# Expert tiles of 32 rows on four column quarters of TensorE, moved on ScalarE's queue, in a hybrid diffusion layer with 16 routed experts

## What is computed

```python
def routed_moe(h, router_w, router_b, w1, w3, w2):
    ...  # sigmoid scores; one of 4 expert groups, then the top 2 of its 4 experts
    gate = jnp.sum(jax.nn.one_hot(idx, N_EXPERTS, dtype=F32) * w[..., None], axis=1).astype(h.dtype)
    out = jnp.zeros_like(h)
    for e in range(N_EXPERTS):                       # 16 experts, w1, w3: 1024x512, w2: 512x1024
        he = jax.nn.silu(h @ w1[e]) * (h @ w3[e])
        out = out + gate[:, e:e + 1] * (he @ w2[e])
    return out
```

## Time and profile before

| | us |
|---|---|
| median of three runs | 1959.97 |
| the profiled execution | 1965.64 |
| its span, first to last instruction | 1964.0 |
| span until the first matmul of the experts (L998) | 1590.4 |
| expert stage, to the end of the last `down` | 333.3 |
| gather, sum, norm and output after it | 40.3 |
| bytes moved in the whole span | 243.50 MB |

### The profile page before, as it was taken

One profiled execution on the slowest core, in us unless ns is written; L12 is line 12 of the kernel. 1 busy time (PEld: TensorE's weight loads), 2 busy tenths in 40 slices (PEclk: granted clock), 3 DMA queues, 4 the chain that ended last, 5 costly groups with the idle time before them and its releaser, 6 DMA issues.

```text
span 1964.0 us, 17655 instructions
## 1 busy us (share of the span) xinstructions
PE 1720.4 (88%) x6784; PEld 945.7 (48%) x6785; DVE 736.4 (37%) x1229; ACT 380.6 (19%) x651; POOL 266.8 (14%) x272
## 2 busy tenths in 40 slices
PE   4988899799789879999999999999999569999791
PEld 0553454355355344544545555446564236666460
DVE  1144644653754554600027774123143312222124
ACT  2321232132132121000123334101100201111111
POOL 0003412421430540000000000000000021111014
PEclk9999989899989889999999999999999879999896
DMA  9611101011021025621120111215205749887974
GB/s 315 253 40 43 43 22 43 4 61 43 1 86 43 0 78 217 219 85 45 49 79 0 43 44 43 86 44 184 86 0 215 264 155 372 308 297 257 379 268 141
DMA packets 108941, 243.50 MB, mean 124 GB/s; under 512 B 7913, under 2 KB 17134, under 8 KB 108882
## 3 DMA queue, kind: packets, MB, share of 16 engines
q1 hardware_dynamic: 86800, 180.59, 26.0%
q0 software_dynamic: 14128, 50.60, 7.4%
q10 hardware_dynamic: 7954, 11.50, 1.6%
HBM read 220.40 MB, written 22.28 MB: 124 GB/s over the span
## 4 chain that ended last, share of the span: by engine, by line
PE 74%; DVE 13%; ACT 4%; issue 3%; POOL 2%; DMA 2%; ACTq 1%; SPq 1%; DVEq 0%; POOLq 0%; PEldq 0%
PE psum L419 15%; PE psum L998 9%; PE psum L431 8%; PE psum L709 6%; PE psum L1023 4%; PE psum L596 4%; PE psum L423 4%; PE psum L824 3%; PE psum L654 2%; PE psum L622 2%; PE psum L493 2%; PE psum L441 2%; PE psum L858 1%; PE psum L756 1%; DVE arena L1621 1%
## 5 line engine op out<-in xcount | busy, mean ns | idle before, releaser
L419 PE MATMUL psum<-arena 128*128 128x512 f32 x688 | 315.2, 615 | 9.7 <-issue 4.0
L419 PEld LDWEIGHTS psum<-arena 128*128 128x128 f32 x688 | 133.3, 197 | 171.9 <-issue 164.1
L998 PE MATMUL psum<-arena 128*64 128x256 f32 x1664 | 190.5, 387 | 10.8 <-DMA arena<-exp_w_d 9.2
L998 PEld LDWEIGHTS psum<-arena 128*64 128x64 f32 x1664 | 144.7, 139 | 62.6 <-issue 29.0
L431 PE MATMUL psum<-arena 128*128 128x512 f32 x352 | 151.6, 592 | 0.0
L596 PE MATMUL psum<-arena 128*128 128x512 f32 x256 | 130.7, 641 | 1.2 <-ACT arena L1172 1.2
L709 PE MATMUL psum<-arena 128*128 128x512 f32 x256 | 111.6, 593 | 0.0
L431 PEld LDWEIGHTS psum<-arena 128*128 128x128 f32 x352 | 66.8, 190 | 83.3 <-issue 83.2
L1023 PE MATMUL psum<-arena 128*64 128x512 f32 x416 | 95.0, 596 | 6.1 <-ACT arena L1439 6.1
L2013 POOL TENSOR_TENSOR arena<-arena 128x512 f32<-128x512 f32 x40 | 49.5, 1247 | 359.4 <-ACT arena L1227 309.2
L2049 POOL TENSOR_TENSOR arena<-arena 128x512 f32<-128x512 f32 x64 | 82.6, 1294 | 103.0 <-ACT arena L1267 103.0
(11 more groups left out here) (340 smaller groups left out, 2096.6 us busy)
## 6 DMA issues: line engine op xcount, KB each, us to landing
arena<-exp_w_d SPq DMA_DIRECT2D x48, 2048.0 KB, 19.1
arena<-w_in_d SPq DMA_DIRECT2D x22, 2048.0 KB, 7.8
arena<-ada_w_d POOLq DMA_DIRECT2D x8, 2048.0 KB, 9.1
slots<-arena POOLq DMA_DIRECT2D x1, 8704.0 KB, 26.3
arena<-ada_w_d SPq DMA_DIRECT2D x4, 2048.0 KB, 23.4
arena<-ssd_proj_d SPq DMA_DIRECT2D x4, 2048.0 KB, 9.8
arena<-slots POOLq DMA_DIRECT2D x28, 256.0 KB, 6.4
slots<-arena POOLq DMA_DIRECT2D x54, 128.0 KB, 5.3
```

The source lines that it names most:

```text
L419: ins = mmul(ps[:, 0:T], slot[:, k, m * P:(m + 1) * P], src[:, k, C:NT], start=(k == 0), stop=(k == KD - 1))
L998: ins = mmul(ps[q * R:(q + 1) * R, 0:HF], XT[:, k, :], w[:, k, q * HF:(q + 1) * HF], start=(k == 0), stop=(k == KD - 1))
```

## The change

Tiles have 32 rows instead of 64. Four tiles' worth of partitions fit, so `up` and `down` use four column quarters of the array: quarter q streams columns q x 128 to (q+1) x 128 of w1 and, in the same call, of w3 (one view `w13` spans both buffers); psG goes, Silu reads the left 128 columns of psU and the product the right ones. `up` has 8 x 4 = 32 calls of 256 columns, `down` 4 x 4 = 16 calls of 256 columns.

A tile's rows lie on all 128 partitions as (quarter of the channels, row): `xrow` is 128 x 256 instead of 64 x 1024, and `ysb` 128 x 256 in place of 128 x 512. So two transposes turn a tile instead of eight, and one turns the activations instead of two.

Loads and stores of the rows move from GpSimd's queue to ScalarE's, into ScalarE's loop, behind its copy: one load and one store for each tile, the latter in one piece. Their side in HBM is a view with the quarter as its outermost dimension, `r (q c) -> q r c` with q = 4.

With 32 rows the experts take 3, 2, 3, 1, 5, 3, 3, 5, 2, 2, 1, 1, 1, 3, 3, 2 tiles, 40 in all. Core of the diff:

```diff
-ROWS_A_TILE = 64
-HF = FF // 2
-XTILES = 2 * T // ROWS_A_TILE + NE + 2
+ROWS_A_TILE = 32
+NQ = P // ROWS_A_TILE
+HF = FF // NQ
+DQ = D // NQ
+XTILES = 2 * T // ROWS_A_TILE + NE + 4
...
+        w13 = [view(off, (2, KD, FF)) for off in (wset0, 0, phase_base)]
...
             def up(p, j):
                 pe.wait_ge(S_("x_ready"), j + 1)
-                for i, (ps, name) in enumerate(((psG, "g_full"), (psU, "u_full"))):
-                    w = wmem[p][i].rearrange("p (k n) -> p k n", k=KD)
-                    for k in range(KD):
-                        for q in range(2):
-                            ins = mmul(ps[q * R:(q + 1) * R, 0:HF], XT[:, k, :], w[:, k, q * HF:(q + 1) * HF],
-                                       start=(k == 0), stop=(k == KD - 1))
-                    ins.then_inc(S_(name), 1)
+                for k in range(KD):
+                    for q in range(NQ):
+                        ins = mmul(psU[q * R:(q + 1) * R, 0:2 * HF], XT[:, k % 2, k // 2, :],
+                                   w13[p][:, :, k, q * HF:(q + 1) * HF], start=(k == 0), stop=(k == KD - 1))
+                ins.then_inc(S_("u_full"), 1)
             def turns(j):
                 pe.wait_ge(S_("xrow_in"), j * 16 + 32)
-                turn_x(0, KD - 3)
+                turn_x()
                 pe.wait_ge(S_("he_ready"), j + 1)
-                for i in range(HF // P):
-                    ins = nc.tensor.transpose(psH[:, i * P:(i + 1) * P], hg[:, i * P:(i + 1) * P], ident)
-                ins.then_inc(S_("h_turned"), 1)
-                turn_x(KD - 3, KD)
+                nc.tensor.transpose(psH[:, 0:P], hg, ident).then_inc(S_("h_turned"), 1)
...
+                for k in range(NQ):
+                    for q in range(NQ):
+                        ins = mmul(psD[q * R:(q + 1) * R, 0:DQ], heT[:, k, :],
+                                   w2[:, k, q * DQ:(q + 1) * DQ], start=(k == 0), stop=(k == NQ - 1))
...
+            quarters = lambda rows: slots[rows, :].rearrange("r (q c) -> q r c", q=NQ)
+            def load_x(rows):
+                act.dma_start(xrow[:, 0:DQ], quarters(rows)).then_inc(S_("xrow_in"), 16)
+            def send_y(rows):
+                act.dma_start(quarters(rows), ysb).then_inc(S_("y_sent"), 16)
...
             with act.Fori(0, n) as j:
-                act.wait_ge(S_("g_full"), j + 1)
-                run(sg, bank(("G",))[:, 0:HF], ACT.Silu).then_inc(S_("g_ready"), 1)
+                act.wait_ge(S_("u_full"), j + 1)
+                run(sg, bank(("U",))[:, 0:HF], ACT.Silu).then_inc(S_("g_ready"), 1)
                 act.wait_ge(S_("h_turned"), j + 1)
-                run(heT, bank(("H",))[:, 0:HF].rearrange("p (b t) -> p b t", t=P), ACT.Copy).then_inc(S_("heT_ready"), 1)
+                run(heT.rearrange("p q r -> p (q r)"), bank(("H",))[:, 0:P], ACT.Copy).then_inc(S_("heT_ready"), 1)
+                act.wait_ge(S_("x_turned"), j + 2)
+                load_x(bass.ds(j * R + 2 * R, R))
+                act.wait_ge(S_("y_ready"), j + 2)
+                send_y(bass.ds(j * R, R))
...
-            with pool.Fori(0, n) as j:
-                pool.wait_ge(S_("x_turned"), j + 2)
-                pool.dma_start(xrow[0:R, :], slots[bass.ds(j * R + 2 * R, R), :]).then_inc(S_("xrow_in"), 16)
-                pool.wait_ge(S_("y_ready"), j + 2)
-                send_y(bass.ds(j * R, R))
```

More of the change, by code:

```diff
@@ L252, in build @@
         g1row = alloc(D)
-        g2half = alloc(D // 2)
-        XT = alloc(KD, ROWS_A_TILE)
+        g2q = alloc(DQ)
+        XT = alloc(DQ // P, NQ, ROWS_A_TILE)
         assert top[0] <= phase_base
@@ L278, in build @@
         hg = alloc(HF)
-        heT = alloc(HF // P, P)
-        ysb = alloc(D // 2)
+        heT = alloc(NQ, ROWS_A_TILE)
+        ysb = alloc(DQ)
         junk2 = xrow
@@ L976, in _ @@
             R = ROWS_A_TILE
-            psG = open_(pe, ("G",), 1, 0, 1)
             psU = open_(pe, ("U",), 1, 1, 2)
@@ L981, in _, with turn_x @@
             psH = open_(pe, ("H",), 1, 4, 5)
[L983 to L988, removed]
+            def turn_x():
+                for i in range(DQ // P):
+                    ins = nc.tensor.transpose(psX[:, i * P:(i + 1) * P], xrow[:, i * P:(i + 1) * P], ident)
+                ins.then_inc(S_("x_turned"), 1)
             def up(p, j):
@@ L1039, in _ @@
             pe.wait_ge(S_("xrow_in"), 16)
-            turn_x(0, KD)
+            turn_x()
             pe.wait_ge(S_("tiles_known"), 1)
@@ L1433, in _ @@
             act.wait_ge(S_("tiles_known"), 1)
-            n = act.value_load(first_tile_i[0:1, NE:NE + 1], min_val=1, max_val=XTILES)
+            n = act.value_load(first_tile_i[0:1, NE:NE + 1], min_val=1, max_val=XTILES - 4)
+            R = ROWS_A_TILE
+            quarters = lambda rows: slots[rows, :].rearrange("r (q c) -> q r c", q=NQ)
[3 more added lines that the diff above has]
+                act.dma_start(quarters(rows), ysb).then_inc(S_("y_sent"), 16)
+            act.wait_ge(S_("y_ready"), 1)
+            send_y(slice((XTILES - 1) * R, XTILES * R))
+            act.wait_ge(S_("x1_ss"), TL)
+            act.wait_ge(S_("x_sent"), 16 * 2 * TL)
+            load_x(slice(0, R))
+            act.wait_ge(S_("x_turned"), 1)
+            load_x(slice(R, 2 * R))
             with act.Fori(0, n) as j:
-                act.wait_ge(S_("g_full"), j + 1)
-                run(sg, bank(("G",))[:, 0:HF], ACT.Silu).then_inc(S_("g_ready"), 1)
+                act.wait_ge(S_("u_full"), j + 1)
+                run(sg, bank(("U",))[:, 0:HF], ACT.Silu).then_inc(S_("g_ready"), 1)
                 act.wait_ge(S_("h_turned"), j + 1)
-                run(heT, bank(("H",))[:, 0:HF].rearrange("p (b t) -> p b t", t=P), ACT.Copy).then_inc(S_("heT_ready"), 1)
+                run(heT.rearrange("p q r -> p (q r)"), bank(("H",))[:, 0:P], ACT.Copy).then_inc(S_("heT_ready"), 1)
[3 more added lines that the diff above has]
+                send_y(bass.ds(j * R, R))
             for t in range(TL):
@@ L1851, in _ @@
                     dve.wait_ge(*is_full((name, j)))
[L1852 to L1856, removed]
+                    if name == "g1":
+                        ins = v.tensor_copy(g1row[:, j * 512:(j + 1) * 512], bank((name, j)))
+                    else:
+                        for q in range(2):
+                            rows = slice((2 * j + q) * ROWS_A_TILE, (2 * j + q + 1) * ROWS_A_TILE)
+                            ins = v.tensor_copy(g2q[rows, :], bank((name, j))[rows, q * DQ:(q + 1) * DQ])
+                    ins.then_inc(is_free((name, j))[0], 1)
             for j in range(2):
@@ L1953, in _ @@
             v.memset(ysb, 0.0).then_inc(S_("y_ready"), 1)
[L1954 to L1955 removed]
+            by_turn = lambda x: x.rearrange("p (q i) -> p i q", i=DQ // P).unsqueeze(3).to_broadcast([P, DQ // P, NQ, R])
+            A2 = by_turn(modA[:, 2, :])
+            B2 = by_turn(mod[:, 3 * KD:4 * KD, 0])
             def modulate_x(n):
                 dve.wait_ge(S_("x_turned"), n)
[L1960 removed]
+                v.tensor_tensor(XT, psX[:, 0:DQ].rearrange("p (i q r) -> p i q r", q=NQ, r=R), A2, ALU.mult).then_inc(S_("x_scaled"), 1)
                 dve.wait_ge(S_("x_scaled"), n)
@@ L1967, in _ @@
                 dve.wait_ge(S_("g_ready"), j + 1)
-                dve.wait_ge(S_("u_full"), j + 1)
-                v.tensor_tensor(hg, sg, psU[:, 0:HF], ALU.mult).then_inc(S_("he_ready"), 1)
+                v.tensor_tensor(hg, sg, psU[:, HF:2 * HF], ALU.mult).then_inc(S_("he_ready"), 1)
                 modulate_x(j + 2)
                 dve.wait_ge(S_("down_full"), j + 1)
-                dve.wait_ge(S_("y_sent"), j * 32 + 32)
-                v.tensor_tensor(ysb, psD[:, :], g2half, ALU.mult).then_inc(S_("y_ready"), 1)
+                dve.wait_ge(S_("y_sent"), j * 16 + 16)
+                v.tensor_tensor(ysb, psD[:, 0:DQ], g2q, ALU.mult).then_inc(S_("y_ready"), 1)
             for t in range(TL):
@@ L2075, in _ @@
             pool.wait_ge(S_("x_sent"), 16 * 2 * TL)
[L2076 to L2088, removed]
-            n = pool.value_load(first_tile_i[0:1, NE:NE + 1], min_val=1, max_val=XTILES - 2)
-            with pool.Fori(0, n) as j:
-                pool.wait_ge(S_("x_turned"), j + 2)
-                pool.dma_start(xrow[0:R, :], slots[bass.ds(j * R + 2 * R, R), :]).then_inc(S_("xrow_in"), 16)
-                pool.wait_ge(S_("y_ready"), j + 2)
-                send_y(bass.ds(j * R, R))
-            pool.wait_ge(S_("y_sent"), n * 32 + 32)
+            n = pool.value_load(first_tile_i[0:1, NE:NE + 1], min_val=1, max_val=XTILES - 2)
+            pool.wait_ge(S_("y_sent"), n * 16 + 16)
             pool.sem_inc(S_("pool_passed"), 1)
```

2 lines of the change are left out of this document (1 added, 1 removed).

## The result

The changed kernel takes 2039.05 us (median of four runs, 2033.83 to 2045.25) against 1957.24 for the kernel before beside it: a ratio of 1.0415, with a 95% interval of 1.0375 to 1.0456. It is slower by 4%, as forecast, and by twice the forecast amount: 82 us where 42 were expected.

A forecast was written before the change was run, and what follows sets the result against it. TensorE's tile loop was taken as the bound, DMA close behind. Rows on four engines delay the last weights to 1953, plus 14 gives 1967 against 1923.7; 1965.6 + 42, less 5.7, gives 2002 us (1975 to 2050; 8 in 10: 1922 to 2050).

The forecast's parts named there:

- The pace of the matmuls: `up` and `down` on four column quarters: 0.054 us per instruction, a period of 7.16 us instead of 12.21.
- rival 2: Quarters in `up` and `down` do not overlap four at once, only two run: stage 495, 2120 us; chance 0.09.
- Four engines: Row loads and stores with outermost size four in HBM work on four DMA engines, always the same four, not 16.
- Rival 1: All 16 engines work on the row transfers, a period of 7.16 holds: stage 301, 1928 us, faster; chance 0.20.
- The cost of rows on the engines: Row transfers: 0.047 us per 1 KB packet, 3.0 us a tile on each of four engines, beside 229 us of weights.
- The landing of a load: Row load under weight traffic: lands in 8 us on four engines, making a period under traffic of 9 to 10 us.
- the bulk sum: Engine time in the expert stage: 1613 + 229 + 37 x 3.0 = 1953 us for last weights, ending at 1967, +43.
- the per-tile view: Tile loop with loads landing in 8 us: 40 x 9.4 = 376 us of stage, 333 + 43.
- The low clock: TensorE may fall to 1.2 GHz after waits of 4 us and more; some 25 us allowed at the range's top.
- What is moved and costs nothing: Row issues moved from GpSimd to ScalarE's queue cost nothing; the table load stays hidden with 0.8 us to spare.

The follow-up runs named there:

- e2: The changed kernel with loads written row outermost and stores cut into four transfers on GpSimd's queue, all on 16 engines: 1940.85 us, 0.9908 of the kernel before.
- e5: The changed kernel with only a quarter of each weight transfer made from expert 3 on: 1923.54 us, one execution.
- e10: The changed kernel with each expert's w2 loaded in two transfers, in 2 KB packets: 2017.89 us, 1.0301 of the kernel before.
- e3: The changed kernel with only the stores cut into four transfers of 32 partitions on GpSimd's queue, loads unchanged: 2016.88 us, one execution.
- e6: The kernel before with its loads and stores issued on ScalarE's queue, shapes unchanged: 1962.70 us, 1.0019 of the kernel before.
- e4: The changed kernel with its loads and stores issued on GpSimd's queue, shapes unchanged: 2000.12 us, 1.0214 of the kernel before.

## Why the prediction was right or wrong

**The pace of the matmuls: right.** 64 instructions take 3.49 us in the chain, 0.054 each as assumed; four quarters are at work at once, and rival 2 falls. The Trainium skill ("TensorE: Matmul & The Clock Gate", "Part 3: Packing small matmuls — row/col tiling") says that MATMULs start and end strictly in order. What the prediction concluded from it, that the second instruction of a call holds up the next quarter, is not so here: in the records of an undisturbed tile four instructions start within 0.05 us, and the next four 0.216 us after the first. Starts and ends are in order in these records; in which order the two instructions of each call were issued they don't tell, so the page's rule itself is not tested. The period came out at 6.95 us where 7.16 was put together: the hand-over between `up` and `down` was 1.51, not 1.67.

**Four engines: right**, by the 320 closing writes, and it is the cause: with 16 the kernel turns from 4.2% slower to 0.9% faster (e2). Rival 1's price of 1928 us for that case was 13 too low. Its stage of 301 left out the expert changes (15 us in e5, which has hardly any other wait), and allowed 12 for the waits for weights, where the three periods around expert 12 alone exceed 6.95 us by 19 in e2. The shorter period, 6.95 instead of 7.16, gave back 8.

**The cost of rows on the engines: the price right, the use of it wrong.** 10504 packets of ScalarE took 7.8% of 16 x 414 us, 0.049 us each (0.047 assumed), and the weights 56.5%, 234 us on each engine (229 assumed). But the sum 1613 + 229 + 111 + 14 took the four engines to be always full. They were busy for 234 + 80 x 32 x 0.049 = 359 of 414 us. What set the stage was the chain of loads, with one wait of 27.4 us for expert 12's weights in it, and not a full engine; e10, with the same bytes on the same four engines, was 19.5 us shorter.

**The landing of a load: mis-sized, and this is the step that failed.** It was 3.7 + 32 x (0.047 + 0.087) = 8 us for a period of 9 to 10. Measured: a lead of 4.0 to 4.1 us to the first packet, a spread of 4.9 beside 2 KB packets and 6.6 beside w2's, and another 0.7 to 0.9 until the semaphore is complete. So a load beside w1 or w3 lands after 10.1 us and one beside w2 after 11.2 to 11.5; the 18 links of the chain average 10.5. Three terms were too small. The fixed part was put at 3.7 and is 5.0. Beside 2 KB packets the turns were put at 4.3 and took 4.9: in those stretches a packet of rows takes 0.054 us and one of weights 0.10 (means), 32 x 0.154 = 4.9, and not 0.047 and 0.087. And beside w2 a turn has a packet of 4 KB (0.165 at the median), which the formula left out. Splitting w2 took 1.0 us off a link (e10), keeping the stores off the same four rings 0.5 (e3: 18 links of 10.0 on average). The chain from load to load adds 0.9 us for the turning and the issue, so a period that waits is 10.5 + 0.9 = 11.4 and more (11.9 measured), not 9 to 10. That the bulk sum and the per-tile view both gave 376 was read as support; it was a coincidence. The bulk sum described no bound. The per-tile view gave all 40 tiles 9.4 us, where 25 took 11.9 and 14 only 7.6: 62 us too little for the first, 25 too much for the others. That the total came as near as it did owes something to this luck.

**The low clock: right to leave it out of the sum.** It came, as in the earlier trace rows, and after shorter waits too, of 2.1 us already, but mostly beside the loads: some 17 us on the chain, of which 3 stand for expert 12's wait as before, within the 25 allowed at the top.

**What is moved and costs nothing: right at 16 engines, wrong at four.** e6 gives 0.2%. The table load stayed hidden with 0.53 us to spare (0.8 assumed):

```profile
1712.66 0.28 ACT L1448 ACTIVATE arena<-psum 128x128 f32<-128x128 f32 x1 [0.53 <-PE psum L996]
```

That the move to another queue would not be free at four engines, where GpSimd's is 39 us better (e4), was left out of the sum. **Not foreseen** either was the expert change, about 0.85 us for most of them.

**What stays open.** The balance of the 58 and 19 us for loads and stores is measured, but how much of the stores' part is `ysb`, how much the ring that they share with loads, and how much the change of queue was not separated at four engines. In e3, with the stores elsewhere, a load beside w2 lands no later (10.0 us) than one beside w1 or w3 (10.2; medians of nine each), so the longer turns cost less there than one for one would give; why stays open. e4's 39 us have three possible sources. The wait for expert 12's weights is in every version, and no run removed it.

## What to carry to other kernels

When a change gives a transfer a small outermost dimension, count its DMA engines before its bytes, on ScalarE's and SyncE's queues by the closing packets under 512 B, and write the view so that the long dimension comes first, or cut the transfer by partitions. A transfer that lies in a loop through a single buffer is paid for by its landing time and not by its bytes: work that out as the lead, plus packets on one engine times the sum of its own packet and the neighbour's, plus the time to the semaphore, with all four read from a stretch under the same traffic. If two estimates of a bound agree, check that each resource in them would really be full.

## What the runs showed of the hardware

- Four column quarters with float32 pairs of instructions keep up 0.054 us for each instruction of 256 columns, a quarter of the 0.215 of the full array; four start within 0.05 us, every 0.216.
- 32 packets of 1 KB on each of four engines need 1.9 us alone, 4.9 us beside 2 KB packets and some 6.6 beside 4 KB ones, as if the packets of two queues took turns whatever their size. The first packet comes after 1.4 us without traffic and after 4.0 to 4.1 with it, and the semaphore is complete 0.4 us behind the last one without traffic and 0.7 to 0.9 with it.
- Transfers on four engines use the same four each time on ScalarE's queue (the last four of the 16 closing writes of a weight transfer come 2.5 us after the others) and changing ones on GpSimd's (0.2 us). GpSimd's queue also puts pieces of 1 KB together into larger packets; ScalarE's leaves them at 1 KB. The two queues differ by 39 us at four engines and by nothing at 16.
- The issue of a load of 128 KB takes ScalarE 0.56 us with the quarter outermost and 0.35 us with contiguous pieces:

```profile
1621.63 0.35 ACTq L1434 DMA_DIRECT2D arena<-slots  x1
```
